# Three row tiles instead of two behind three of the norms of a two-block layer kernel

## What is computed

```python
def rmsnorm(x, g):
    y = x * lax.rsqrt(jnp.mean(x * x, axis=-1, keepdims=True) + EPS)
    return y * g
# first block
z = rmsnorm(h, g_mix) @ w_in                 # q, k, v of 12 heads, u, two gates
q = partial_rotary(q, positions); k = partial_rotary(k, positions)
outs, lses = dilated_band_attention(q, k, v, ...)        # three groups
y = gelu(s5_ssm(u, ...))
h = h + (gate_attn * attn_d + gate_ssm * ssm_d) @ w_out
...
# second block
h = rmsnorm(x, norm1_g) * (1.0 + scale1) + shift1
proj = h @ w_in                              # x_rnn 1280, q_lat, kv_lat, k_rope, g_rnn, g_mla
xc = causal_dwconv(x_rnn, conv_w, conv_b)
r = sigmoid(xc_blocks @ w_a + b_a); i = sigmoid(xc_blocks @ w_x + b_x)
a = exp(-8 * r * softplus(-lru_param)); h_t = a_t * h_{t-1} + sqrt(1 - a_t ** 2) * (i * xc)
...
h2 = rmsnorm(x, norm2_g) * (1.0 + scale2) + shift2
u = causal_dwconv(h2 @ w_up, ffn_conv_w, ffn_conv_b)
x = x + gate2 * ((silu(u_gate) * u_val) @ w_down)
```

## Time and profile before

| what | value |
|---|---|
| median of three runs | 1807.0 us (1806.66 to 1809.52) |
| span of the profiled execution | 1806.3 us |
| TensorE busy | 1790.0 us |
| VectorE, ScalarE, GpSimd busy | 1042.5, 788.0, 266.3 us |
| memory traffic | 202 MB, 112 GB/s |

### The profile page before, as it was taken

How to read it: one execution, slowest core, us unless ns; L and a number is a source line. 1 busy time by engine, 2 the same in 40 slices (tenths; PEclk the granted TensorE clock), 3 DMA queues, 4 the chain that set the end, 5 groups by cost and what they waited for, 6 DMA issues and landing times.

```text
span 1806.3 us, 21066 instructions
## 1 busy us (share of the span) xinstructions
PE 1790.0 (99%) x8198; PEld 1425.8 (79%) x8198; DVE 1042.5 (58%) x1554; ACT 788.0 (44%) x1248; POOL 266.3 (15%) x349
## 2 busy tenths in 40 slices
PE   9999999999999999999999999999999999999998
PEld 7888888878887888888887678766668788888887
DVE  8755544765566544554478796255545675435543
ACT  6544444524344222222264666355643454224443
POOL 4766536200000000000001110322110000000000
PEclk9999999999999999999999999999999999999999
DMA  6222222134344545554341422311133232323231
GB/s 216 94 88 88 68 85 87 56 116 152 93 144 154 194 144 183 202 186 152 117 139 56 133 87 85 132 65 58 36 125 120 82 105 94 94 93 94 93 94 70
DMA packets 65411, 202.07 MB, mean 112 GB/s; under 512 B 7520, under 2 KB 11872, under 8 KB 65312
## 3 DMA queue, kind: packets, MB, share of 16 engines
q1 hardware_dynamic: 65312, 200.72, 33.6%
HBM read 192.30 MB, written 8.40 MB: 111 GB/s over the span
## 4 chain that ended last, share of the span: by engine, by line
PE 94%; DVE 3%; ACT 2%; issue 0%; DMA 0%; SPq 0%; POOL 0%; ACTq 0%; DVEq 0%; POOLq 0%
PE bank L254 28%; PE bank L256 28%; PE bank L255 28%; PE bank L662 2%; PE bank L692 1%; PE bank L677 1%; PE bank L300 1%; PE bank L343 1%; PE bank L359 1%; DVE wlo L1463 1%; PE bank L540 1%; ACT whi L861 1%; PE bank L389 0%; PE bank L380 0%; PE bank L296 0%
## 5 line engine op out<-in xcount | busy, mean ns | idle before, releaser
L254 PE MATMUL bank<-tiler,whi 128*128 128x512 f32 x2260 | 908.7, 402 | 5.1 <-DVE wlo L1463 2.3
L256 PE MATMUL bank<-tiler,wlo 128*128 128x512 f32 x2260 | 893.2, 395 | 0.0
L255 PE MATMUL bank<-tiler,whi 128*128 128x512 f32 x2260 | 892.6, 395 | 0.0
L861 ACT ACTIVATE whi<-raw 128x1024 fp32r<-128x1024 f32 x284 | 298.7, 1053 | 518.5 <-PE bank L256 515.8
L254 PEld LDWEIGHTS bank<-tiler,whi 128*128 128x128 f32 x2260 | 426.9, 189 | 121.3 <-issue 20.4
L256 PEld LDWEIGHTS bank<-tiler,wlo 128*128 128x128 f32 x2260 | 426.2, 189 | 99.9
L255 PEld LDWEIGHTS bank<-tiler,whi 128*128 128x128 f32 x2260 | 426.8, 189 | 94.9 <-issue 1.7
L1463 DVE TENSOR_TENSOR wlo<-raw,whi 128x1024 fp32r<-128x1024 f32 x263 | 323.1, 1233 | 265.3 <-ACT whi L861 265.0
L2292 POOL TENSOR_TENSOR stat<-stat,scl 128x4 f32<-128x4 f32 x7 | 7.5, 1080 | 749.3 <-DVE stat L1976 428.2
L2283 POOL TENSOR_TENSOR wlo<-raw,whi 128x1024 fp32r<-128x1024 f32 x21 | 49.9, 2375 | 217.4 <-ACT whi L861 217.4
L2231 DVE SCALAR_TENSOR_TENSOR tile<-bank,sm,tile 128x511 f32<-128x511 f32 x42 | 31.5, 750 | 85.8 <-ACT tile L1427 54.1
(11 more groups left out here) (384 smaller groups left out, 1602.4 us busy)
## 6 DMA issues: line engine op xcount, KB each, us to landing
raw<-wst SPq DMA_DIRECT2D x284, 512.0 KB, 3.6
wide<-wadaT SPq DMA_DIRECT2D x52, 512.0 KB, 3.4
tile<-xT SPq DMA_DIRECT2D x16, 256.0 KB, 6.2
spare<-tile SPq DMA_DIRECT2D x16, 256.0 KB, 2.2
tile<-spare SPq DMA_DIRECT2D x16, 256.0 KB, 6.2
out<-tile SPq DMA_DIRECT2D x8, 256.0 KB, 2.5
tile<-gblk SPq DMA_DIRECT2D x5, 256.0 KB, 4.6
us<-tile SPq DMA_DIRECT2D x4, 256.0 KB, 2.0
```

Source lines behind the costliest of these rows:

```text
L254: e.matmul(bank, whi[:, o:o + 128], hi, start=start, stop=False)
L255: e.matmul(bank, whi[:, o:o + 128], lo, start=False, stop=False)
L256: e.matmul(bank, wlo[:, o:o + 128], hi, start=False, stop=stop).then_inc(*sig("blk", n))
L861: e.activation(whi[:, c % NHL * W:(c % NHL + 1) * W], raw[:, c % NRAW * W:(c % NRAW + 1) * W], ACT.Copy).then_inc(*sig("hi", c))
```

## The change

Three row tiles take each operand behind the three norms: q, k and v of the first head group in the first block (`in` 0, 12 and 24; v goes into bank 4, which is free once u's first tile is copied), `in2` 2, 3 and 4 in the second block, and `up` 1, 23 and 2. The copies of the raw row tiles move from behind the eight operands to behind the first. Chunk halves are made at other operands (k = 1 and 4 on ScalarE, 3 and 6 on VectorE). The LRU's gates, sigmoids, tanh and maximum come one row tile later, and its last exp falls behind the next chunk. The number and the sizes of all instructions stay as they are. The diff, cut to its core:

```diff
+            def proj3(a, b, c, ops, need, freed_by=None):
+                for k in range(len(ops)):
+                    proj(*a, ops, [k], 0, need)
+                    proj(*b, ops, [k])
+                    if freed_by and k == 0:
+                        e.wait_ge(*at(*freed_by))
+                    proj(*c, ops, [k])
...
-                            proj2("in", 0, B[0], "in", 12, B[1], N1, "n1")
+                            proj3(("in", 0, B[0]), ("in", 12, B[1]), ("in", 24, B[4]), N1, "n1", ("u_raw", 0))
                         continue
-                    if s == 2:
-                        e.wait_ge(*at("u_raw", 2))
-                    else:
-                        e.wait_ge(*free_a(s - 2))
-                    bank = B[6 if s == 2 else s % 2]
+                    e.wait_ge(*free_a(s - 2))
+                    bank = B[s % 2]
...
-            proj2("in2", 2, ba, "in2", 3, bb, NN, "nn")
+            proj3(("in2", 2, ba), ("in2", 3, bb), ("in2", 4, bank("conv", 4)), NN, "nn")
             spread("r1", 30, B[7])
-            for m in range(4, 24):
+            for m in range(5, 24):
...
-                if m < 14:
-                    gate_rnn(m - 4)
+                if m < 15:
+                    gate_rnn(m - 5)
...
+                    if m == 1:
+                        proj3(("up", 1, bank2(2, "cv_g", 1)), ("up", 23, bank2(3, "cv_u", 1)), ("up", 2, bank2(4, "cv_g", 2)), N1, "n3")
+                    elif m == 2:
+                        proj("up", 24, bank2(5, "cv_u", 2), N1)
...
-                    if m == 1:
-                        proj2("up", m, ba, "up", 22 + m, bb, N1, "n3")
...
                     if name == "n1":
-                        if k in (1, 3, 4, 6):
-                            u_raw((0, 0, None, 1, 2, None, 3)[k])
+                        if k in (0, 3, 4, 6):
+                            u_raw((0, None, None, 1, 2, None, 3)[k])
...
-                if k in (1, 7):
+                if k == 0:
+                    for i in range(2):
+                        e.wait_ge(*made("in2", i))
+                        e.activation(F(48 + i), B[i], ACT.Copy).then_inc(*sig("raw", i))
+                if k in (1, 4):
                     prep(first.get(("in2", 0), 0) + 8 * (k // 4 + 1))
-            for i in range(2):
-                e.wait_ge(*made("in2", i))
-                e.activation(F(48 + i), B[i], ACT.Copy).then_inc(*sig("raw", i))
...
-                if 4 <= m <= 13:
-                    lru_sigmoids(m - 4)
                 if 5 <= m <= 14:
-                    lru_tanh(m - 5)
+                    lru_sigmoids(m - 5)
+                if 6 <= m <= 15:
+                    lru_tanh(m - 6)
...
                 if m == 15:
-                    for i in range(5, 10):
+                    for i in range(5, 9):
                         lru_exp(i)
                 if m == 16:
+                    lru_exp(9)
                     for i in range(5):
                         lru_sqrt(i)
...
-            prep(first.get(("up", 0), 0))
+            prep(first.get(("up", 0), 0) + 8)
...
-                if k in (1, 7):
-                    prep(first.get(("up", 0), 0) + 8 * (k // 4 + 1))
-            for i in range(2):
-                e.wait_ge(*made("up", 22 * i))
-                e.activation(F(70 + i), B[i], ACT.Copy).then_inc(*sig("raw2", i))
+                if k == 0:
+                    for i in range(2):
+                        e.wait_ge(*made("up", 22 * i))
+                        e.activation(F(70 + i), B[i], ACT.Copy).then_inc(*sig("raw2", i))
+                if k in (1, 4):
+                    prep(first.get(("up", 0), 0) + 8 * (k // 4 + 2))
...
             def modulated(name, rb, w, ops, so, sh, ahead):
                 for k in range(9):
-                    if k == 3:
-                        prep(ahead)
+                    if k in (3, 6):
+                        prep(ahead + (0 if k == 3 else 8))
...
-                if 6 <= m <= 15:
-                    lru_max(m - 6)
+                if 7 <= m <= 16:
+                    lru_max(m - 7)
```

More of the change, by code:

```diff
@@ L218, in program, with up_at @@
         first, done = {}, {}
+        def up_at(m, x):
+            return first.get(("up", 0), 0) + 16 * m + 8 * x if m in (1, 2) else first.get(("up", m + 22 * x), 0)
         def made(name, m):
@@ L431, in tensor @@
                     m = part * 12 + a % 3 * 4 + a // 3 if a < 12 else 40 + s - 36
-                    if a == 0 and part < 2:
+                    if a == 0:
                         if part == 0:
-                            proj2("in", 0, B[0], "in", 12, B[1], N1, "n1")
+                            proj3(("in", 0, B[0]), ("in", 12, B[1]), ("in", 24, B[4]), N1, "n1", ("u_raw", 0))
                         continue
-                    if s == 2:
-                        e.wait_ge(*at("u_raw", 2))
-                    else:
-                        e.wait_ge(*free_a(s - 2))
-                    bank = B[6 if s == 2 else s % 2]
+                    e.wait_ge(*free_a(s - 2))
+                    bank = B[s % 2]
                     proj("in", m, bank, N1, range(4))
@@ L814, in tensor @@
                 for m in range(11 * hf if hf else 1, 11 * hf + 11):
-                    ba, bb = bank2(p, "cv_g", m), bank2(p + 1, "cv_u", m)
-                    p += 2
-                    if m == 1:
-                        proj2("up", m, ba, "up", 22 + m, bb, N1, "n3")
-                    else:
-                        proj("up", m, ba, N1)
-                        proj("up", 22 + m, bb, N1)
+                    if m == 1:
+                        proj3(("up", 1, bank2(2, "cv_g", 1)), ("up", 23, bank2(3, "cv_u", 1)), ("up", 2, bank2(4, "cv_g", 2)), N1, "n3")
+                    elif m == 2:
+                        proj("up", 24, bank2(5, "cv_u", 2), N1)
+                    else:
+                        proj("up", m, bank2(p, "cv_g", m), N1)
+                        proj("up", 22 + m, bank2(p + 1, "cv_u", m), N1)
+                    p += 2
                 ba, bb = bank2(p, "h_dn", hf, 0), bank2(p + 1, "h_dn", hf, 1)
@@ L993, in scalar @@
                     e.wait_ge(*made("in", 24 + b % 3 * 4 + b // 3))
-                    e.activation(perm(F(VT[b % 2]), d), nat(B[(3 * b + 2) % 2 if b else 6], d), ACT.Copy).then_inc(*sig("v_sb", b))
+                    e.activation(perm(F(VT[b % 2]), d), nat(B[(3 * b + 2) % 2 if b else 4], d), ACT.Copy).then_inc(*sig("v_sb", b))
                 if a > 12:
@@ L1032, in scalar @@
                 if a < 12:
-                    start_of("in", 24 + m0)
+                    prep(first.get(("in", 24 + m0), 0) if a else 6 * CB)
                     e.wait_ge(*made("in", 12 + m0))
@@ L1406, in scalar @@
                     if m:
-                        prep(first.get(("up", m), 0) + (8 if m < 4 else 0))
+                        prep(up_at(m, 0) + (8 if m < 4 else 0))
                     if m % 11:
@@ L1419, in scalar @@
                     if m:
-                        prep(first.get(("up", 22 + m), 0) + (16 if m == 1 else 8 if m < 4 else 0))
+                        prep(up_at(m, 1) + (8 if m < 4 else 0))
                     e.wait_ge(*at("cv_g", m))
@@ L1518, in modulated @@
                                                in1=R(hi).bitcast(F32), op0=ADD, op1=SUB).then_inc(*sig("oplo", name, k - 1))
-                prep(ahead + 8)
             def sincos(kind, src, tmp):
@@ L1582, in vector @@
             e.tensor_copy(maskb[:, :], F(64)[:, 128:512]).then_inc(*sig("masks"))
-            start_of("in", 24)
+            prep(6 * CB)
             e.wait_ge(*at("sin", 1))
@@ L2221, in vector @@
             variance("n3", B[6], 1024, ST_N3)
+            prep(first.get(("up", 0), 0) + 8)
             diagonal("n3", ST_N3, 25)
             e.wait_ge(*at("rb", "n3"))
-            modulated("n3", B[7], CU, N1, S_N2, 24, first.get(("up", 0), 0) + 8)
+            modulated("n3", B[7], CU, N1, S_N2, 24, first.get(("up", 0), 0) + 16)
             for i in range(2):
@@ L2525, in load_u @@
                         *sig("u4", j, r, by=16))
-            until("in", 24)
+            chunks(12)
             for j in range(4):
```

## The result

The changed kernel takes 1819.7 us (median of 5 runs, 1819.57 to 1821.08) against 1807.4 of the kernel before, run beside it (5 runs, 1806.66 to 1809.52). The ratio is 1.0067, 95% interval 1.0055 to 1.0078: slower beyond the 0.2% line, and above the range of 1807.6 to 1815.5. The profiled execution has a span of 1817.8 us against 1806.3, that is +11.5 where the sum said +5.3.

The account below looks back on a forecast made before the run. TensorE, busy 1790 of 1806.3 us, bounds the kernel. First norm +1.9, second block's first norm +0.5, LRU's end +1.2, last norm +1.7 sum to 5.3: 1811.6, plus 0.7 for the median, rounded to 1812; range 1807.6 to 1815.5.

Follow-up runs that it names:

- experiment 9: Kernel before with the first block's part of the change alone, GpSimd's scaling of u held back until k's rotation is done: 1808.5 us against 1806.9.
- experiments 1: Kernel before with the first block's part of the change alone: 1813.0 us against 1808.1.
- 2: Kernel before with the part of the second block's first norm and the LRU's shift alone: 1810.8 us, ratio 1.0018.
- 5: Changed kernel with SyncE's two chunk loads put back between the first and second store of the residual: 1816.5 us.
- 8: Kernel before with three row tiles behind the second block's two norms only, two chunk loads put back, chunk halves one place sooner: 1805.1 us against 1807.5.
- 10: Same as experiment 9, with q and k of the first head group in each other's banks: 1809.8 us, ratio 1.0016.
- experiment 12: Kernel before with 8 unread matmuls of constants ahead of each of its two 1.9 us waits followed by a slow clock: 1806.6 us against 1806.9.

## What to carry to other kernels

When a change shifts a chain in time, look up what every other engine does in the new time slot, GpSimd's long operations above all, before its durations are carried over. Compare two orders only at points at which the same instructions are done. And read the price of an idle from several executions: one profile tells that the clock can fall, not how often.

## What the hardware showed

**An idle of 2 us costs 1.5 us in clock, or nothing.** Over all 14 traces TensorE had 20 idles of 1.8 to 2.0 us from the first norm on. 13 of them were followed by a stretch at 1.2 GHz, 7 by none. Of five idles of 2.1 to 2.4 us four were, of four of 3.6 us all, and of those up to 1.3 us none. There is nothing in between: where the clock stayed up, the next 23 matmuls took the same time within 0.03 us from trace to trace at the same place, and where it fell 1.45 to 1.59 us more. It is not the place: here is the same wait behind r1's diagonal (1.91 and 1.92 us), first in the kernel before, then in experiment 9.

```profile
971.50:975.50 4.00, 4.00 (x12) 3.10 (x12) 3.83 (x6) 0.00 (x0) 0.00 (x0) 0.59 0.00 0
```

```profile
971.50:975.50 4.00, 4.00 (x17) 2.90 (x17) 3.89 (x6) 0.00 (x0) 0.00 (x0) 1.00 0.01 2
```

The Trainium skill, "TensorE: Matmul & The Clock Gate", section "What's actually happening", says that the number of slow matmuls differs from run to run. The traces agree that the same wait has them in one run and not in another (5 to 8 of the 128x512 ones, or none, behind the 1.8 to 2.0 us), but the time lost is nearly the same each time it is lost. What chooses in a given execution, no run here shows.

**A second, smaller effect.** In 8 of the 14 traces matmuls start 0.2324 us apart through all the long stretches (start to start in the timeline, averaged over some 170 at a time). In six (experiments 1, 2, 5, 8, 10, 12) they start 0.2333 apart for one feed-forward part, some 360 to 400 us, at a granted clock of 1.00: 1.6 us in all. It isn't tied to the change, since experiment 12 is the kernel before with 16 matmuls more and has it. Its cause is open. It is as large as a slow stretch, and spans of single traces should not be compared more closely than this.
